# Modulation blocks of a two-layer diffusion trunk: the four partial rows summed by one-pass matmuls of a high and a low row, the split made on VectorE, and the turn behind the third tile of four in the FFN

## The reference, cut to what matters

```python
def adaln(cvec, w, b):
    m = jax.nn.silu(cvec) @ w + b
    return jnp.split(m, N_MOD, axis=-1)
...
    mc = adaln(c_ctx, ada_w[l], ada_b[l])
    ml = [t[:, None, :] for t in adaln(c, ada_w[l], ada_b[l])]
    hc = modulate(xc, norm_mix[l], mc[0], mc[1])
    ...
    xc = xc + mc[2] * yc
    hc = modulate(xc, norm_ffn[l], mc[3], mc[4])
    xc = xc + mc[5] * conv_ffn(hc, ffn_w_in[l], ffn_conv_w[l], ffn_conv_b[l], ffn_w_out[l])
```

## Time and profile before

| | |
|---|---|
| time, median of 3 runs (lowest, highest) | 2006.08 us (2005.9, 2007.87) |
| the profiled execution, its own time | 2007.44 us |
| its span, first to last instruction | 2005.6 us |
| TensorE busy | 1967.7 us, 98% of the span |
| VectorE, GpSimd, ScalarE busy | 1011.5, 784.1, 657.1 us (50%, 39%, 33%) |
| granted TensorE clock, mean | 0.999 |

### The profile page before, as it was taken

How to read it: one execution, slowest core, us unless ns; L and a number is a source line. 1 busy time by engine, 2 the same in 40 slices (tenths; PEclk the granted TensorE clock), 3 DMA queues, 4 the chain that set the end, 5 groups by cost and what they waited for, 6 DMA issues and landing times.

```text
span 2005.6 us, 28323 instructions
## 1 busy us (share of the span) xinstructions
PE 1967.7 (98%) x10558; PEld 1652.8 (82%) x10558; DVE 1011.5 (50%) x1434; ACT 657.1 (33%) x1233; POOL 784.1 (39%) x543
## 2 busy tenths in 40 slices
PE   7999999999999999999999999998999999999998
PEld 4887888888788878898888898895578998998996
DVE  3323530442353057672565375766635773674575
ACT  6332223213222225321232233435545331232232
POOL 4343333234323425333333333446865333333332
PEclk9999999999999999999999999999999999999999
DMA  8421332232133213432433222510013322222221
GB/s 346 172 74 63 127 116 94 95 116 74 63 126 116 74 34 125 157 108 81 147 116 115 74 74 74 187 64 6 1 53 127 126 74 78 79 69 79 74 73 53
DMA packets 53556, 195.70 MB, mean 98 GB/s; under 512 B 5968, under 2 KB 7376, under 8 KB 52432
## 3 DMA queue, kind: packets, MB, share of 16 engines
q1 hardware_dynamic: 48096, 174.68, 25.4%
q10 hardware_dynamic: 5360, 19.65, 2.6%
HBM read 187.23 MB, written 7.08 MB: 97 GB/s over the span
## 4 chain that ended last, share of the span: by engine, by line
PE 90%; DVE 3%; ACT 2%; issue 2%; POOL 2%; DVEq 1%; DMA 1%; POOLq 0%; SPq 0%; ACTq 0%
PE ps L555 20%; PE ps L510 19%; PE ps L525 16%; PE ps L503 7%; PE ps L491 5%; PE ps L504 4%; PE ps L747 4%; PE ps L776 3%; PE ps L587 2%; PE ps L505 1%; ACT pr L1370 1%; PE ps L418 1%; DVE front L1584 1%; POOL pr L1557 1%; PE ps L609 1%
## 5 line engine op out<-in xcount | busy, mean ns | idle before, releaser
L1438 POOL TENSOR_TENSOR w_l<-raw,w_h 128x1024 fp32r<-128x1024 f32 (+1 forms) x240 | 572.5, 2389 | 1013.4 <-ACT w_h L1071 1013.4
L1071 ACT CAST w_h<-raw 128x1024 fp32r<-128x1024 f32 x232 | 244.6, 1055 | 523.6 <-PE ps L555 271.2
L510 PE MATMUL ps<-hx,w_h 128*128 128x384 f32 x1472 | 375.3, 335 | 0.0
L525 PE MATMUL ps<-w_h,hx 128*128 128x512 f32 x960 | 299.9, 391 | 0.0
L510 PEld LDWEIGHTS ps<-hx,w_h 128*128 128x128 f32 x1472 | 268.2, 188 | 4.1
L510 PE MATMUL ps<-hx,w_l 128*128 128x384 f32 x736 | 247.0, 336 | 0.0
L503 PE MATMUL ps<-hx,w_h 128*128 128x512 f32 x644 | 231.7, 398 | 0.0
L525 PEld LDWEIGHTS ps<-w_h,hx 128*128 128x128 f32 x960 | 180.2, 188 | 40.9 <-issue 3.6
L504 PE MATMUL ps<-hx,w_l 128*128 128x256 f32 x736 | 191.1, 280 | 0.0
L525 PE MATMUL ps<-w_l,hx 128*128 128x512 f32 x480 | 186.9, 389 | 0.0
L1629 DVE TENSOR_TENSOR ps<-ps,gate 128x512 f32<-128x512 f32 x110 | 76.2, 693 | 219.2 <-PE ps L555 219.0
(11 more groups left out here) (232 smaller groups left out, 3181.2 us busy)
## 6 DMA issues: line engine op xcount, KB each, us to landing
raw<-stream_dram SPq DMA_DIRECT2D x312, 512.0 KB, 3.3
first_w<-first_dram SPq DMA_DIRECT2D x16, 512.0 KB, 15.5
gate<-gate_b_dram ACTq DMA_DIRECT2D x4, 1024.0 KB, 4.8
S<-state_dram ACTq DMA_DIRECT2D x4, 1024.0 KB, 7.5
new_state_dram<-st_out ACTq DMA_DIRECT2D x8, 512.0 KB, 5.2
xt<-x_dram ACTq DMA_DIRECT2D x5, 512.0 KB, 9.7
y_dram<-front SPq DMA_DIRECT2D x5, 512.0 KB, 2.6
rope_t<-rope_t_dram ACTq DMA_DIRECT2D x4, 512.0 KB, 3.5
```

The costliest lines, as they stand in the source:

```text
L510: mm = nc.tensor.matmul(ps[:, banks + 1, 0:REST], w, x[:, k, HALF:T], start=(k == 0 and n == 0), stop=(k == KT - 1 and n == 2))
L525: mm = nc.tensor.matmul(ps[:, bank(t), 0:n_cols], x[:, k, t * P:(t + 1) * P], w, start=(k == 0 and n == 0), stop=(k == KT - 1 and n == 2))
L1071: nc.scalar.copy(w_h[:, r, :], raw[:, s, :]).then_inc(hi_ready[r], 1)
L1438: op = nc.gpsimd.tensor_tensor(w_l[:, r, at], raw[:, s, at], w_h[:, r, at].bitcast(F32), ALU.subtract)
```

## The change

Two columns of the constant table are added: C_BOTH selects rows 32g+s and 32g+2+s for condition s, C_LOW is -1 on the rows 32g+2+s and 0 elsewhere. `csil` gets the two condition rows twice (columns 0, 1 and 2, 3), so that each partial sum stands in PSUM on two partitions. For all blocks but the four of the opening and the first of each of `first_tiles` (three), the evacuation is a copy to float32r on all rows and then one operation that leaves the rounded value on the upper rows and the rest on the lower ones, both on VectorE; the turn then adds eight rows with float32r operands. ScalarE's `ada_copy` goes away in these places and stays in `first_tiles`, where nothing else is changed. In the FFN the evacuation stands ahead of tile (0,1) on VectorE, the turn behind tile (1,0) on TensorE, and `ada_mods` or `gate_add` ahead of tile (1,1) on VectorE; the first GATE part keeps its places.

```diff
@@ csil: the condition rows twice
+            nc.scalar.activation(csil[:, :, 2:4], cvec, ACT.Silu)
             nc.scalar.activation(csil[:, :, 0:2], cvec, ACT.Silu).then_inc(csil_ready, 1)
...
-            def ada_turn(par, copied):
+            def ada_turn(par, copied, whole=False):
 
                 pe.wait_ge(ada_copied, copied)
+                rows, to = (ada_o, sel) if whole else (ada_r, sel_r[:])
                 for f in range(4):
                     mm = nc.tensor.matmul(ps[:, 4 + par, 2 * f:2 * f + 2],
-                                          ada_o[:, f * P:(f + 1) * P], sel, start=True, stop=True)
+                                          rows[:, f * P:(f + 1) * P], to, start=True, stop=True)
...
-            def gate_turn(par, copied):
+            def gate_turn(par, copied, whole=False):
 
                 pe.wait_ge(ada_copied, copied)
+                rows, to = (ada_o, sel) if whole else (ada_r, sel_r[:])
                 for s in range(2):
-                    mm = nc.tensor.matmul(ps[:, 4 + par + s, :], sel[:, s:s + 1].to_broadcast([P, P]), ada_o[:],
+                    mm = nc.tensor.matmul(ps[:, 4 + par + s, :], to[:, s:s + 1].to_broadcast([P, P]), rows[:],
                                           start=True, stop=True)
...
-                                    if mode and q == 0 and w == 1:
-                                        (gate_turn if mode == GATE else ada_turn)(0, ada0 + i + 1)
+                                    if mode and (q, w) == ((0, 1) if first else (1, 0)):
+                                        (gate_turn if mode == GATE else ada_turn)(0, ada0 + i + 1, first)
...
-                            if mode == GATE and part > 0:
-                                ada_copy(b, 0, i, 4)
...
-                                    if mode == TURN and q == 0 and w == 0:
-                                        ada_copy(b, 0, i, 4)
...
-                if j == 2:
-                    ada_copy(b, 4, 0, 4)
...
-                V.tensor_copy(ada_o[:], ps[:, 4 + par, :]).then_inc(ada_copied, 1)
+                if b is None:
+                    V.tensor_copy(ada_o[:], ps[:, 4 + par, :]).then_inc(ada_copied, 1)
+                    return
+                V.tensor_copy(ada_r[:], ps[:, 4 + par, :])
+                dve.drain()
+                V.scalar_tensor_tensor(out=ada_r[:], in0=ada_r[:].bitcast(F32), scalar=cst[:, C_LOW:C_LOW + 1],
+                                       in1=ps[:, 4 + par, :], op0=ALU.mult, op1=ALU.add).then_inc(ada_copied, 1)
...
+            dve.wait_ge(const_in, 16)
+            V.tensor_copy(sel_r[:], cst[:, C_BOTH:C_BOTH + 2])
...
-                                    if mode == TURN and q == 0 and w == 1:
+                                    if q == 0 and w == 1 and (mode == TURN or mode == GATE and part > 0):
+                                        ada_copy(b, 0, i, 0)
+                                    if mode == TURN and q == 1 and w == 1:
                                         ada_mods(0, ada0 + i + 1, ada0 - 4 + i)
-                                    if mode == GATE and q == 0 and w == 1:
+                                    if mode == GATE and (q, w) == ((1, 1) if part > 0 else (0, 1)):
                                         gate_add(0, ada0 + i + 1, 1 + 2 * l, slice(part * 512, part * 512 + 512))
...
             for j in range(10):
+                if j == 3:
+                    ada_copy(SEG["att"], 4, 0, 0)
```

More of the change, by code:

```diff
@@ L50 @@
 C_ID, C_SEL, C_ZF, C_ZB = 0, 128, 130, 131
-C_W = 132
+C_BOTH, C_LOW = 132, 134
+C_W = 135
 V_C, V_ADAB, V_NORM, V_DEC, V_SINK = 0, 16, 80, 112, 120
@@ L227, in build @@
         csil = sb("csil", [P, KT, 32])
-        ada_o = sb("ada_o", [P, 512])
+        with ExitStack() as whole:
+            ada_o = sb("ada_o", [P, 512], F32, whole)
+        ada_r = sb("ada_r", [P, 512], F32R)
+        sel_r = sb("sel_r", [P, 2], F32R)
         gate = sb("gate", [P, 2, D])
@@ L624, in _ @@
             norm_turn(0, 0, (0,))
-            ada_turn(0, 1)
+            ada_turn(0, 1, True)
             norm_turn(0, 1, (0,))
@@ L630, in _ @@
             warm(4, 0)
-            ada_turn(0, 2)
+            ada_turn(0, 2, True)
             warm(10, 0)
@@ L640, in opening @@
                 first_low(b, 0, range(0, 4))
-                ada_turn(0, 3)
+                ada_turn(0, 3, True)
                 first_high(b, 1, range(0, 4))
@@ L644, in opening @@
                 first_low(b, 1, range(0, 4))
-                ada_turn(0, 4)
+                ada_turn(0, 4, True)
                 for t in range(TT):
@@ L908, in _ @@
             first_tiles(b, 2, 6, ATT_ADA)
-            gate_turn(0, ATT_ADA + 1)
+            gate_turn(0, ATT_ADA + 1, True)
             for j in range(2, 10):
@@ L1833, in ffn_phase @@
                         ada0 = FFN_ADA[l].get((g, part))
+                        b = SEG["in", l, g, part]
                         def pair_group(i):
@@ L2055, in _layout @@
             cst[32 * g + s, C_SEL + s] = 1
+            cst[[32 * g + s, 32 * g + 2 + s], C_BOTH + s] = 1
+            cst[32 * g + 2 + s, C_LOW] = -1
     cst[:, C_ZF], cst[:, C_ZB] = P - 1 - i, i
```

## The result

The changed kernel takes 2019.45 us (median of 5 runs, 2016.33 to 2020.81) against 2006.13 us (median of 5): it is 13.3 us slower, with a ratio of the means of 1.0062, 95% interval [1.0051, 1.0073]. The ratios leave out one execution of the kernel before that took 3965.0 us and one of run 10 that took 3941.33 us. Forecast was 4.5 us more, in a range up to 2015; the direction was right, the size was not. The profiled execution took 2019.45 us with a span of 2017.7.

A forecast was written before the change was run, and what follows sets the result against it. TensorE, busy 1967.7 of 2005.6 us, was taken to bound the kernel. Second GATE parts +10.6, TURN ends +1.4, heads -4.9, attention -1.0, other TURN turns -1.6 give +4.5 on 2006.08: 2010.6 us, range 2005.0 to 2015.0.

The forecast's parts named there:

- The turns: On TensorE: a gate turn falls from 1.72 to 0.46 us, a column turn from 0.79 to 0.40 us.
- Heads and attention: Cheaper turns with the evacuation hidden in the heads save 4.9 us there; the attention saves 1.0 us.
- The attention's turn: TensorE waits 0.3 us there for VectorE's evacuation, leaving 1.0 of the 1.26 us saved.
- The ends of the TURN parts: TensorE waits about 1.1 us for the column addition at the end of both TURN parts of FFN 0.
- the TURN parts as a whole: Four turns inside their loops gain 1.6 us; the last of each part loses 0.7 us, 1.4 in all.
- the place of the stall: Second GATE parts: TensorE stalls behind tile (1,1) for the gate addition, 5.5 us in FFN 0; both parts lose 10.6 us.
- the wait at the turn: Second GATE parts: TensorE waits about 0.9 us at the turn behind tile (1,0) for VectorE's evacuation.
- the second stretched step of tile (0,0): Second GATE part: GpSimd's earlier subtractions meet both convolution steps, each 2.87 us, a second delay of 2.0 us.
- The step that failed: Second GATE part, FFN 0: VectorE starts its sum at 826.3, takes as long as before, ends convolution (1,0) at 838.0.
- rival B: TensorE's clock falls in the stalls, 3.5 us more each: 2014 us at one, 2017.6 at both; chance 0.20.
- Rival C: Second GATE parts: GpSimd's subtractions don't meet both steps, loss 6.6 us in place of 10.6, 2006.6 us; chance 0.22.
- Rival D: Ends of parts: VectorE adds gate and columns before tile (1,1) ends, all 10.8 us saved, 1995.3 us; chance 0.05.

The follow-up runs named there:

- run 10: Changed kernel with columns and gates added between sum and convolution of tile (1,0), and the copy of the second GATE block back on ScalarE: 1996.87 us.
- run 2: Kernel before with the change in the retention heads and the attention alone, both FFNs as before: 1999.47 us.
- run 4: Changed kernel with 24 matmuls into an unused bank ahead of the wait at the end of both second GATE parts: 2013.10 us.
- run 1: Changed kernel with the second GATE part of each FFN put back as before (ScalarE copy, float32 turn, addition ahead of the second sum): 2000.21 us.
- run 3: Kernel before with only the second GATE part's places moved (turn behind tile (1,0), addition ahead of (1,1)), copy still on ScalarE: 2016.12 us.
- run 5: Changed kernel with GpSimd subtracting only 128 of 1024 columns in the second GATE parts (output wrong there): 1999.40 us.
- run 9: Changed kernel with second GATE parts as before and, in the TURN parts, columns added between sum and convolution of tile (1,0): 1996.52 us.
- runs 6 and 8: Changed kernel, TensorE waiting for the gate only at the bank's next use: 2004.41 us; also GpSimd subtracting 128 of 1024 columns in FFN 1's blockless part: 2000.63 us.

## Why the forecast was wrong

**Right, with their sizes.** The turns: 0.47 and 0.34 us, forecast 0.46 and 0.40. Heads and attention: 6.9 us by run 2, forecast 5.9. The attention's turn did not wait in run 2 or in the changed kernel; it waited 0.55 us in run 4 and 0.38 in run 10, forecast 0.3. The ends of the TURN parts: 0.96 and 0.93 us, forecast 1.1, and the TURN parts as a whole nothing that run 1 and run 2 can tell apart, forecast -0.2. In the GATE parts the place of the stall, the wait at the turn, and the second stretched step of tile (0,0): VectorE begins its sum of (0,1) 7.8 us behind TensorE's end of that tile (819.32 against 811.57), forecast 7.9.

**The step that failed** is the sentence that VectorE's "way from there to the end of the convolution of (1,0) ... is as long as before". From the start of the sum of (0,1) it was 11.7 us before (823.91 to 835.61) and is 13.2 us now (819.32 to 832.51). The convolution of (1,0) has two stretched steps in place of the one of the earlier trace rows, 1.9 us more; 0.4 us come back in tile (0,1), whose first step took 0.99 us before and takes 0.61 now. The cause lies on the other two engines, where ScalarE rounds the chunks that GpSimd then subtracts. Before, ScalarE and GpSimd in the pair of (1,0):

```profile
830.34 1.06 ACT L1071 CAST w_h<-raw 128x1024 fp32r<-128x1024 f32 x1
834.08 0.38 ACT L1310 COPY ca<-ps 128x256 f32<-128x256 f32 x1 [2.68 <-PE ps L510]
...
831.48 2.48 POOL L1438 TENSOR_TENSOR w_l<-raw,w_h 128x1024 fp32r<-128x1024 f32 x1 [6.42 <-ACT w_h L1071]
835.86 2.40 POOL L1438 TENSOR_TENSOR w_l<-raw,w_h 128x1024 fp32r<-128x1024 f32 x1 [1.90 <-ACT w_h L1071]
```

After, ScalarE at the same place (GpSimd is the row of 826.51 above):

```profile
825.37 1.06 ACT L1077 CAST w_h<-raw 128x1024 fp32r<-128x1024 f32 x1
827.19 0.37 ACT L1315 COPY ca<-ps 128x256 f32<-128x256 f32 x1 [0.76 <-PE ps L514]
```

ScalarE waits for VectorE's product ahead of each pair. When VectorE is late, ScalarE waits for the second tile of the pair only 0.76 us and not 2.68, it rounds the two chunks 2.5 us apart (825.37 and 827.83) and not 4.4 (830.34 and 834.72), and GpSimd's two subtractions follow each other and cover two steps of the convolution. I had found this order in tile (0,0) and had not asked whether the lateness makes it again one pair on. These 1.5 us make 7.0 us of the 5.5; smaller differences, among them 0.4 us from the end of the addition to the first matmul, cancel.

**The term left to a rival** is the clock. It fell in both stalls, as in rival B at both (2017.6), to which I gave a small part of 0.20. I had asked for "the stalls at their full length"; run 3 shows it fall behind 3 us. So the forecast put the clock at nothing, and it cost some 5.3 us. The price of 3.5 us a stall was too high: 5.5 us at half speed lose 2.7, and run 4 gets back about that. With 2 x 1.5 for the stalls and 5.3 for the clock the forecast of 2010.6 becomes 2018.9, against 2019.45 measured. Its two sides fit too: the two parts lose 10.6 + 3.0 + 5.3 = 18.9 us, against 19.2 by run 1, and the rest gains 4.9 + 1.0 + 1.6 - 1.4 = 6.1, against 6.0.

**What did not decide.** Rival C (GpSimd misses one step) was wrong in its sign: GpSimd met more steps, not fewer. Rival D's condition, that the convolution of (1,0) comes 1.3 us ahead of the end of the part, holds in run 5 (in FFN 0 827.05 against 828.50), and its 1995.3 is near what run 9 reached by another way.

## What to carry to other kernels

Before work is put on an engine that is off the critical path, ask what its lateness does to the engines that share something with it: here an evacuation of 1.5 us on VectorE, in place of a copy on ScalarE, brought two more of VectorE's steps together with GpSimd's operations. A stall of 3 us (run 3) became one of 7, and the lateness did not go away by itself. An operation that somebody waits for goes ahead of long work on its engine, not behind it (run 9); a wait that is moved later helps in full only if the engine waited for can get level again (runs 6 and 8). Price every wait of the busiest engine with the clock that it may cost behind it.

## What the runs showed of the hardware

The granted clock was 0.50 for 5.5 us of work behind idleness of 7.0 us, and it fell behind 2.98 and 3.01 us too (run 3), in the first of these cases only at 836.5, when TensorE had worked again for 1.2 us; behind 1.58 us (run 4) it stayed at 1.00. The Trainium skill (page "TensorE: Matmul & The Clock Gate", section "Why this matters for your kernels") warns of idle gaps between bursts of matmuls, and the rows agree; the price in each case is from the rows here.

In the attention the profiled execution of the changed kernel shows a longer wait for a table than any other, 11.02 us against 5.95 to 7.40. VectorE, start, duration, idle before:

```profile
1281.39 0.53 DVE L1900 TENSOR_SCALAR nsink<-vec 128x16 f32<-128x16 f32 x1 [11.02 <-DMA ck<-cache_k_dram]
```

TensorE stood still for 2.47 us behind it (2.5 in the waits above) and ran at the lower level from about 1290.2 to 1293.6. In the profiled executions of the nine other kernels with the same attention it stands there for 0.55 us, so it seems to belong to that execution; why the table came late is open, and so is how often it happens in the runs that were only timed.

Traces also differ in the opening by over 2 us without any change in the code: the first product of the kernel before starts at 29.69 us in its own trace, and at 27.52 us in that of run 3, which has the same program up to there. TensorE in the kernel before:

```profile
18.50 1.09 PE L461 MATMUL ps<-cst,front 128*128 128x128 f32 x4
...
29.69 0.36 PE L434 MATMUL ps<-hx,w_h 128*128 128x256 f32 x1 [0.18 <-ACT hx L1113]
```

In run 3:

```profile
18.02 0.64 PE L461 MATMUL ps<-cst,front 128*128 128x128 f32 x4
...
27.52 0.36 PE L434 MATMUL ps<-hx,w_h 128*128 128x256 f32 x1 [0.18 <-ACT hx L1113]
```

The same four matmuls take 1.09 and 0.64 us, and the granted clock reads 1.00 from 18 to 20 us in both traces, so what slows them is open. A difference of that size between two single traces is therefore read only behind the opening.
